# Two gate projections of a three-layer block as one tile, and weight rooms split into halves

## What is computed

```python
h = rmsnorm_2(x, g_mix)
proj = h @ w_in
fox_qkv, fox_f, sc_bcv, dn_qkv, dn_b, dn_a, dn_z, br_gate = split_cols(proj, IN_SIZES)
y_fox = forgetting_attention(fq, fk, fv, fox_f, b_fox_f, fox_q_gain, fox_k_gain)
#   log_f = log_sigmoid(f_logit + b_f); cum_f = cumsum(log_f); logits get cum_f[q] - cum_f[k]
y_sc = sb * causal_dwconv(sc * sv, sc_conv_w)
dn_qkv = silu(causal_dwconv(dn_qkv, dn_conv_w))
beta = sigmoid(dn_b)
g = -exp(dn_a_log) * softplus(dn_a + dn_dt_bias)
o_dn = gated_delta_rule(l2norm(dq), l2norm(dk_), dv_, g, beta)
```

## Time and profile before

| | us |
|---|---|
| three timed runs | 2346.04, 2346.47 (median), 2348.34 |
| profiled execution | 2348.38 |
| its span in the trace | 2345.5 |
| TensorE busy | 2289.0 (98%) |
| VectorE busy | 1129.4 (48%) |
| ScalarE busy | 870.5 (37%) |
| GpSimd busy | 386.5 (16%) |
| stage `mix` | about 1238 to 1310 |
| stage `fox` | about 1310 to 1374 |
| stage `dn` | 1374 to about 1635 |
| longest wait of TensorE for VectorE (line 1233, first block) | 6.0 |

### The profile page before, as it was taken

The page is one execution under the profiler, slowest core; times in us unless marked ns, Lnnn a source line. Parts: engine busy times, 40 slices in busy tenths (PEclk is TensorE's granted clock), DMA queues, the critical chain, the costliest instruction groups (busy, mean ns, idle before and its releaser), DMA issues.

```text
span 2345.5 us, 26129 instructions
## 1 busy us (share of the span) xinstructions
PE 2289.0 (98%) x10864; PEld 1855.9 (79%) x10864; DVE 1129.4 (48%) x1726; ACT 870.5 (37%) x1290; POOL 386.5 (16%) x339
## 2 busy tenths in 40 slices
PE   7899999999999999999999999999999999999998
PEld 6467888888876678888888878888888788888887
DVE  4974433434224645344346656554333346555553
ACT  5574221223224643122143465442322233333243
POOL 1431110112200012011031303332001111000020
PEclk9799999999999999999999999999999999999999
DMA  3303323223351022332346142225255332332332
GB/s 128 108 1 112 104 90 105 93 90 105 97 162 45 1 72 90 102 96 90 107 82 91 18 45 56 54 46 81 65 96 92 90 108 81 100 108 90 91 108 62
DMA packets 221955, 197.05 MB, mean 84 GB/s; under 512 B 5216, under 2 KB 215596, under 8 KB 221709
## 3 DMA queue, kind: packets, MB, share of 16 engines
q1 hardware_dynamic: 219820, 189.70, 30.8%
q0 software_dynamic: 1504, 5.51, 0.7%
q10 hardware_dynamic: 513, 0.17, 0.0%
HBM read 190.65 MB, written 4.72 MB: 83 GB/s over the span
## 4 chain that ended last, share of the span: by engine, by line
PE 90%; DVE 5%; ACT 3%; DMA 1%; issue 1%; ACTq 0%; POOL 0%; DVEq 0%; POOLq 0%
PE bank L525 24%; PE bank L527 24%; PE bank L526 24%; PE bank L2175 5%; PE bank L848 3%; PE bank L2361 2%; PE bank L1662 1%; PE bank L1489 1%; DVE dsa_latents L1179 1%; PE bank L699 1%; DVE small L1177 1%; PE bank L832 1%; PE bank L709 1%; PE bank L2052 1%; DVE weight_lo L511 1%; DMA weight_raw<-in_w_in 1%
## 5 line engine op out<-in xcount | busy, mean ns | idle before, releaser
L525 PE MATMUL bank<-h_hi,weight_hi 128*128 128x512 f32 x1576 | 619.6, 393 | 6.2 <-DVE h_lo L631 3.6
L527 PE MATMUL bank<-h_hi,weight_lo 128*128 128x512 f32 x1576 | 615.3, 390 | 0.0
L526 PE MATMUL bank<-h_lo,weight_hi 128*128 128x512 f32 x1576 | 614.9, 390 | 0.0
L511 DVE TENSOR_TENSOR weight_lo<-weight_raw,weight_hi 128x2048 fp32r<-128x2048 f32 (+2 forms) x182 | 385.0, 2115 | 382.6 <-ACT weight_hi L502 382.6
L502 ACT ACTIVATE weight_hi<-weight_raw 128x2048 fp32r<-128x2048 f32 (+2 forms) x183 | 321.4, 1756 | 359.2 <-PE bank L527 316.0
L525 PEld LDWEIGHTS bank<-h_hi,weight_hi 128*128 128x128 f32 x1576 | 296.4, 188 | 70.9 <-issue 7.4
L527 PEld LDWEIGHTS bank<-h_hi,weight_lo 128*128 128x128 f32 x1576 | 296.4, 188 | 63.1
L526 PEld LDWEIGHTS bank<-h_lo,weight_hi 128*128 128x128 f32 x1576 | 296.7, 188 | 61.7 <-issue 0.2
L525 PE MATMUL bank<-hidden_hi,weight_hi 128*128 128x512 f32 x512 | 201.8, 394 | 0.0
L527 PE MATMUL bank<-hidden_hi,weight_lo 128*128 128x512 f32 x512 | 200.7, 392 | 0.0
L526 PE MATMUL bank<-hidden_lo,weight_hi 128*128 128x512 f32 x512 | 198.7, 388 | 0.0
(11 more groups left out here) (411 smaller groups left out, 3155.1 us busy)
## 6 DMA issues: line engine op xcount, KB each, us to landing
weight_raw<-in_w_down SPq DMA_DIRECT2D x40, 1024.0 KB, 5.1
weight_raw<-in_w_up SPq DMA_DIRECT2D x32, 1024.0 KB, 5.4
weight_raw<-in_w_up SPq DMA_DIRECT2D x44, 512.0 KB, 5.1
weight_raw<-in_w_in SPq DMA_DIRECT2D x20, 1024.0 KB, 9.0
weight_raw<-in_w_in SPq DMA_DIRECT2D x26, 512.0 KB, 6.8
weight_raw<-in_w_kv_shared SPq DMA_DIRECT2D x6, 1024.0 KB, 5.0
weight_raw<-in_w_branch SPq DMA_DIRECT2D x6, 1024.0 KB, 5.0
weight_raw<-in_a_w_o SPq DMA_DIRECT2D x4, 1024.0 KB, 6.5
```

The source lines that it names most:

```text
L511: dve.e.tensor_tensor(split_flat(v, 1), raw_flat(v), f32(split_flat(v, 0)), ALU.subtract).then_inc(*split.mark(("unit", v)))
L525: pe.e.matmul(o, w[0], x[0], start=start, stop=False)
L526: pe.e.matmul(o, w[0], x[1], start=False, stop=False)
L527: return pe.e.matmul(o, w[1], x[0], start=False, stop=stop)
```

## The change

1. The unit and tile `dn_b` are gone. The unit `fox_f` now reads two ranges of 32 columns, `fox_f`'s and those of `dn_b` and `dn_a`, by two DMAs; its tile has 64 rows. Rows 0 to 7 are the forget gates, rows 32 to 39 the delta rule's.
2. In `mix`, ScalarE copies rows 32 to 39 out of PSUM, TensorE transposes them after fox tile 3, and VectorE multiplies them by the token factors of the norm (the projections of this stage are taken from the unnormed stream), to `ba_cols`. In `dn`, sigmoid and softplus start from `ba_cols`. The wait for the normed stream moves to the first delta rule tile.
3. `weight_raw`, `weight_hi` and `weight_lo` have four halves of 1,024 columns. `lay_out` gives a unit one or two halves in turn and lists the units that held them before; load and rounding wait for those. The loads have four semaphores instead of two, and a load also waits for unit u - 4.
4. At the start of `dn`, ScalarE and VectorE round and split up to the unit of ("dn", 0, 2) ahead of the softplus chain; before, up to that of ("dn", 0, 0).

The diff, cut to its core:

```diff
-    plan.insert(len(plan) - 5, (("fox_f", 0), (w, 0, NC, [(IN_F, IN_F + P)], True)))
-    add(("dn_b",), w, 0, NC, IN_B, IN_B + P)
+    plan.insert(len(plan) - 5, (("fox_f", 0), (w, 0, NC, [(IN_F, IN_F + 32), (IN_B, IN_B + 32)], True)))
...
-        raw_units = sbuf("weight_raw", P, N_RAW, UNIT_COLUMNS)
-        unit_pair = pair("weight", N_SPLIT, UNIT_COLUMNS)
+        raw_units = sbuf("weight_raw", P, N_RAW * UNIT_COLUMNS)
+        unit_pair = pair("weight", N_SPLIT * UNIT_COLUMNS)
...
-        raw_in = [signal(f"weight_in{n}") for n in range(N_RAW)]
+        raw_in = [signal(f"weight_in{n}") for n in range(2 * N_RAW)]
...
+        def lay_out(units, slots):
+
+
+            half_columns, at, last, where, before = UNIT_COLUMNS // 2, 0, [None] * (2 * slots), {}, {}
+            for u in units:
+                kc, width = unit_shape(u)
+                size = 1 if kc * width <= half_columns else 2
+                at = at + at % 2 if size == 2 else at
+                halves = [(at + n) % (2 * slots) for n in range(size)]
+                before[u] = sorted({last[n] for n in halves} - {None})
+                for n in halves:
+                    last[n] = u
+                where[u] = halves[0] * half_columns
+                at = (at + size) % (2 * slots)
+            return where, before
+
+        raw_at, raw_before = lay_out(range(len(plan)), N_RAW)
+        split_at, split_before = lay_out(halved, N_SPLIT)
...
-            if u >= N_RAW:
-                if plan[u - N_RAW][1][4]:
-                    sp.wait_ge(*split_by(u - N_RAW).when("unit", u - N_RAW))
+            for v in raw_before[u] + ([u - 2 * N_RAW] if u >= 2 * N_RAW else []):
+                if plan[v][1][4]:
+                    sp.wait_ge(*split_by(v).when("unit", v))
                 else:
-                    free, name = raw_free.get(u - N_RAW, (split, "none"))
+                    free, name = raw_free.get(v, (split, "none"))
                     sp.wait_ge(*free.when(*name))
...
-                    before = halved.index(v) - N_SPLIT
-                    act.wait_ge(*raw_in[v % N_RAW].when("unit", v))
-                    if before >= 0:
-                        act.wait_ge(*tile_full.when("unit", halved[before]))
+                    act.wait_ge(*raw_in[v % (2 * N_RAW)].when("unit", v))
+                    for before in split_before[v]:
+                        act.wait_ge(*tile_full.when("unit", before))
...
+        ba_rows, ba_cols = step(ATT + 15 * T, T)[32:40, :], small[:, 320:352].rearrange("p (t n) -> p t n", t=NT)
...
-            product_tile(pe, ("fox_f", 0), unit_at["fox_f", 0], 0, h_chunk, (mix.dve, ("forget",)))
+            u = unit_at["fox_f", 0]
+            bank = open_bank(pe, ("fox_f", 0), (mix.dve, ("forget",)), (mix.act, ("ba_rows",)))
+            pe.wait_ge(*split.when("unit", u))
+            for k in range(NC):
+                done = matmul3(pe, bank[0:64, :], columns(u, k, 0, 64), h_chunk(k), k == 0, k == NC - 1)
+            done.then_inc(*tile_full.mark(("fox_f", 0), ("unit", u)))
...
+                if t == 3:
+                    bank = open_bank(pe, ("ba",), (mix.dve, ("ba",)))
+                    pe.wait_ge(*mix.act.when("ba_rows"))
+                    for n in range(NT):
+                        done = pe.e.transpose(bank[:, 8 * n:8 * n + 8], ba_rows[:, n * P:(n + 1) * P], ident[32:40, 32:40])
+                    done.then_inc(*mix.pe.mark(("ba",)))
...
+            act.wait_ge(*tile_full.when("fox_f", 0))
+            act.e.activation(ba_rows, banks.of("fox_f", 0)[32:40, :], ACT.Copy).then_inc(*mix.act.mark(("ba_rows",)))
...
+            dve.wait_ge(*mix.pe.when("ba"))
+            dve.e.tensor_tensor(ba_cols, banks.of("ba")[:, 0:32].rearrange("p (t n) -> p t n", t=NT),
+                                mix_factor.unsqueeze(2).broadcast_to([P, NT, 8]), ALU.mult).then_inc(*mix.dve.mark(("ba",)))
...
+                if item == ("dn", 0, 0):
+                    pe.wait_ge(*fox.dve.when("h", k))
...
-            product(pe, ("dn_b",), h_chunk, lambda t: (dn.act, ("ba_rows",)), lambda k: (fox.dve, ("h", k)))
             tensor_slot(pe, ("open", 0))
-            bank = open_bank(pe, ("ba",), (dn.dve, ("x16",)), (dn.act, ("beta",)))
-            pe.wait_ge(*dn.act.when("ba_rows"))
-            for t in range(NT):
-                done = pe.e.transpose(bank[:, 8 * t:8 * t + 8], ba_rows[:, tiles[t]], ident[0:8, 0:8])
-            done.then_inc(*dn.pe.mark(("ba",)))
...
-            round_upto(act, unit_at["dn_b", 0] + 1)
-            act.wait_ge(*tile_full.when("dn_b", 0))
-            act.e.activation(ba_rows, banks.of("dn_b", 0)[0:8, :], ACT.Copy).then_inc(*dn.act.mark(("ba_rows",)))
+            round_upto(act, item_unit(("dn", 0, 2)))
             scalar_slot(act, ("open", 0))
-            act.wait_ge(*dn.pe.when("ba"))
-            act.e.activation(heads4(beta), banks.of("ba")[:, 0:32].rearrange("p (t n) -> p t n", t=NT)[:, :, 0:4], ACT.Sigmoid
-                             ).then_inc(*dn.act.mark(("beta",)))
+            act.wait_ge(*mix.dve.when("ba"))
+            act.e.activation(heads4(beta), ba_cols[:, :, 0:4], ACT.Sigmoid).then_inc(*dn.act.mark(("beta",)))
...
-            split_upto(dve, unit_at["dn_b", 0] + 1)
+            split_upto(dve, item_unit(("dn", 0, 2)))
             vector_slot(dve, ("open", 0))
-            ba = banks.of("ba")[:, 0:32].rearrange("p (t n) -> p t n", t=NT)
-            dve.wait_ge(*dn.act.when("beta"))
+            dve.wait_ge(*mix.dve.when("ba"))
             dve.wait_ge(*misc_in.when("dn_bias"))
-            dve.e.tensor_tensor(heads4(x16), ba[:, :, 4:8], dt_bias.unsqueeze(1).broadcast_to([P, NT, DN_HEADS]), ALU.add
+            dve.e.tensor_tensor(heads4(x16), ba_cols[:, :, 4:8], dt_bias.unsqueeze(1).broadcast_to([P, NT, DN_HEADS]), ALU.add
```

More of the change, by code:

```diff
@@ L450, in build_program @@
         halved = [u for u, (_, what) in enumerate(plan) if what[4]]
-        split_slot = {u: n % N_SPLIT for n, u in enumerate(halved)}
         raw_free = {}
@@ L456, in unit_shape, with raw_view @@
             return kc, sum(c1 - c0 for c0, c1 in ranges)
-        def raw_view(u):
-            kc, width = unit_shape(u)
-            return raw_units[:, u % N_RAW, 0:kc * width].rearrange("p (k n) -> p k n", k=kc)
+        def lay_out(units, slots):
[13 more added lines that the diff above has]
+        split_at, split_before = lay_out(halved, N_SPLIT)
         def raw_flat(u):
             kc, width = unit_shape(u)
-            return raw_units[:, u % N_RAW, 0:kc * width]
+            return raw_units[:, raw_at[u]:raw_at[u] + kc * width]
+        def raw_view(u):
+            return raw_flat(u).rearrange("p (k n) -> p k n", k=unit_shape(u)[0])
         def split_flat(u, half):
             kc, width = unit_shape(u)
-            return unit_pair[half][:, split_slot[u], 0:kc * width]
+            return unit_pair[half][:, split_at[u]:split_at[u] + kc * width]
         def columns(u, k, c0, c1):
@@ L485, in load_unit @@
                                w[r0:r0 + kc * P, c0:c1].rearrange("(k p) n -> p k n", p=P)
-                               ).then_inc(*raw_in[u % N_RAW].mark(("unit", u), by=16))
+                               ).then_inc(*raw_in[u % (2 * N_RAW)].mark(("unit", u), by=16))
                 at += c1 - c0
@@ L1041, in dsa_tensor @@
             u = unit_at["uk", 0]
-            pe.wait_ge(*raw_in[u % N_RAW].when("unit", u))
+            pe.wait_ge(*raw_in[u % (2 * N_RAW)].when("unit", u))
             for half in range(2):
@@ L1282, in up @@
                 pe.wait_ge(*att0.act.when("o_lat", h))
-                pe.wait_ge(*raw_in[uv % N_RAW].when("unit", uv))
+                pe.wait_ge(*raw_in[uv % (2 * N_RAW)].when("unit", uv))
                 pe.e.matmul(bank, raw_view(uv)[:, 0, h * P:(h + 1) * P], o_lat[h % 2], start=True, stop=True
@@ L2141, in build_program @@
         gcum, to_end, e_end, bexp = dnv[:, 128:144], dnv[:, 144:160], dnv[:, 160:176], dnv[:, 176:192]
-        ba_rows = Kd[:, 0].rearrange("p t n -> p (t n)")[0:8, :]
         ends = dnv[:, 224:240]
```

## The result

The changed kernel takes **2334.11 us** (median of four; 2331.5 to 2335.11), the kernel before 2346.41 beside it: ratio 0.9942, 95% interval 0.993 to 0.9955, some 12 us less. Beside other runs it took 2334.65 where before took 2347.17 (0.9948, 0.9935 to 0.9961). The profiled execution of after took 2331.5 us, span 2329.7; it is the fastest of its four, while that of before, 2348.38 us, stands above all four timed ones (2346.04 to 2348.34).

What follows compares the result with a forecast made beforehand. TensorE was taken as the bound, 90% of the last chain. An earlier `dn` chain (-11.1), moved transposes (+0.5) and full clock behind the remaining wait (-2.4) gave -13.0: 2333.5 us against the median, range 2330.8 to 2341.3.

Steps and rivals of the forecast that it cites:

- The tile and the gates: Opening of `dn`: the 24 matmuls of `dn_b`, 5.57 us on TensorE's path, vanish; the narrower `fox_f` tile costs nothing.
- The moved transposes: Four small transposes move from `dn` into the fox stage: -0.5 us there, +0.5 us here.
- The load of `fox_f`: Before the fox stage: two DMAs of 128 byte pieces land in 5.6 to 26.5 us; taken as no cost.
- The softplus chain: Opening of `dn`: `dt_bias` lands in 3.2 us, the chain runs 1379.5 to 1384.3, silu (0, 0) starts 11.1 us earlier.
- What is late next: Before ("sc", 0, 1): TensorE resumes 11.1 us earlier, at 1401.8, still waiting about 1.4 us instead of 2.73.
- The clock behind it: Behind the wait before ("sc", 0, 1): the granted clock holds instead of halving, another -2.4 us.
- A: The forecast itself: clock holds behind the remaining wait before ("sc", 0, 1), 2333.5 us; chance 0.46.
- B: Rival: the clock falls again behind the remaining wait, so only 10.6 us are saved, 2335.9 us; chance 0.27.
- the step that took the wait's length as what decides: Before ("sc", 0, 1): waits of 1.81 and 2.73 us brought half clock, one of 2.00 did not, so 1.4 should not.
- the one on the early layout: First block: `uv` and first `a_o` loads start earlier, meeting the bias transfer; TensorE's longest wait covers it; nothing taken.
- What halves are good for: Weight rooms in `dn`: four units loaded ahead instead of two, ending ScalarE's 3.59 us idle for the ("sc", 0, 0) load.
- rival C: `dn` chain no earlier relative to TensorE (late `dt_bias` DMAs or tap delayed by roundings); only tile matmuls go, 2341.1 us; chance 0.13.

Runs made afterwards that it cites:

- e10: The changed kernel itself, traced and timed again, nothing altered: 2334.65 us, ratio 0.9948 to the kernel before.
- e12: Changed kernel with the load of `fox_f` in eight DMAs of 1,024 pieces of 32 bytes instead of two of 128 byte pieces: 2335.21 us, one run.
- e5: Changed kernel with weight rooms in halves only from `fox_f` on, earlier units keeping whole slots: 2336.21 us, ratio 0.9955 to the kernel before.
- e11: Changed kernel with VectorE making the first branch's low halves earlier, between the second and third normed head: 2330.94 us, ratio 0.994 to the kernel before.
- e3: Changed kernel without the rounding ahead: one unit rounded and split at the opening of `dn` instead of three: 2335.41 us, ratio 0.9949 to the kernel before.
- e1: Changed kernel reduced to the merged gates: whole weight slots, only the first delta rule unit rounded ahead: 2341.86 us, ratio 0.9976 to the kernel before.
- e9: e1 with the two small DMAs of `a_log` and `dt_bias` issued one stage earlier, at the start of fox attention: 2341.62 us, ratio 0.9977 to the kernel before.

## Why the prediction was right, and where it was not

- **The tile and the gates.** -5.57 and nothing for the narrower tile: the 64 column matmuls take 389 to 397 ns. The moved transposes: +0.5 was said for the way from `mix` to `dn`; to the first tile of the stage it is 125.98 instead of 125.43 us, +0.55. ScalarE's copy took 0.59 us at 1257.24, the product 0.18, neither waited for.
- **The load of `fox_f`.** Two DMAs of 3.9 and 6.1 us, both landed 6.5 us behind the first issue, where 26.5 was the upper bound; TensorE didn't wait. "DMA: Bandwidth & Descriptors", Specifications, in the Trainium skill wants pieces of at least 512 bytes for full rate. The traces agree as to the rate: 512 KB in pieces of 512 bytes took 5.6 us, 256 KB in pieces of 128 bytes 6.5, in pieces of 32 bytes 16.3. What was too high was the prediction's reading that the load would near its upper bound by that rule.
- **The softplus chain.** Said: Abs 5.2 us behind the first tile, silu (0, 0) 13.1. Measured: 4.77 and 12.66; `dt_bias` landed in 2.7 us, not 3.2. The 1.38 us of drain of "ScalarE: Activation LUTs", What ACT_TABLE_LOAD costs, in the Trainium skill, show in no row: from Abs to the last Exp, 1377.03 to 1381.61, it is 4.58 us, with three loads of 1.28, as before.
- **What is late next.** Said: TensorE is there 26.1 us behind the first tile and waits 1.4. Measured: 27.07 - 0.91 = 26.16, and 0.91. The step held, and what it is off by is the landing of `dt_bias`: the wait is 0.88 to 0.97 us where that DMA took 2.7 to 2.8 us (after, e10, e12), and 1.44 and 1.57 where it took 3.3 and 3.4 (e5, e11). The prediction had 3.2 and 1.4.
- **The clock behind it.** Said: -2.4. From the end of that wait to the pair products it was 9.11 us, it is 6.70: -2.41. As A said, and not B; in the three traces with a wait of 0.9 (after, e10, e12) the clock held. But by the runs above, the step that took the wait's length as what decides was weak, and that A came and not B is in part luck: the wait of 1.33 us in e3 and that of 1.81 in the kernel before were followed by the fall, others up to 2.12 were not.
- **In all**, from `mix` to the sums, -13.3, where -13.0 was said.
- **The step that failed** is the one on the early layout: `uv` and the first `a_o` load "meet the transfer of the bias", the wait behind "covers it. I take nothing". The wait's end did stay at 112.1. What was not asked is what a shorter wait does to the clock behind it: 1.1 to 2.8 us.
- **What halves are good for.** The prediction gave them ScalarE's 3.59 us. e1 and e9 show more: with whole slots and `dn_b` gone, the load of ("dn", 0, 2), 11.2 us, is in flight when `dt_bias` is fetched, and rival C's delay, held unlikely because the DMAs "would have to be 5 us later than the row says", is nearly there (7.6 us, against the row's 3.2). In the changed kernel it did not happen: that load is issued at 1309, and the one in flight at 1374 is of ("sc", 0, 1), 6.8 us, and lands at 1375.8. The row of 3.2 was taken beside such a short load too; that another unit's load would stand there was not asked.
- 13.3 + 2.75 is more than the 12 to 13 us between the medians, and both traces are of executions at the edge, a slow one of before and the fastest of after. Single executions differ by falls of the clock of 1.7 us; that this makes the rest is argued, not shown. That the median came so near to 2333.5 is therefore in part luck: the sum from `mix` on was right, the gain in block 1 was missing from it, and the medians show less than the traces.

## What to carry to other kernels

When you remove work ahead of a prefetched chain, ask whether its loads are issued early enough for the new pace: alone, the removed tile turned at once into a wait of nearly the same length. Ask too which load will be in flight when a small DMA is issued, and how long that one takes. Read the clock behind each wait of TensorE together with the wait; shortening a wait whose end another engine sets can still pay, by the clock behind it. And look for operations like the four subtractions of `branch_lo` that stand behind the last step of a stage though their input has long been there.

## What was not expected of the hardware

- A fall of the granted clock behind a wait cost 1.5 to 1.8 us in most traces, in `dn`, in `merge` and in block 1 (2.8 to 3.1 behind the waits of 5.9 to 6.1 us in block 1 and once in `dn`), and came behind one and the same wait of 2.00 us in five traces of twelve.
- A DMA of 2 KB landed in 2.6 to 3.5 us beside a weight load of 512 KB that took 6.5 to 6.9 us, and in 5.6 to 7.6 us beside one that took 10.4 to 11.3; `dt_bias` landed 0.3 to 1.8 us behind that load in thirteen traces.
- Loads of the same size and shape (1,024 rows of 512 bytes) took 6.4 to 6.7 us or 10.7 to 11.6, by the unit they fetch: ("dn", 0, 1), where no other was in flight, the one, ("dn", 0, 2) the other.
- The same 256 KB landed within 6.5 us of the first issue in 2,048 pieces of 128 bytes, within 16.3 us in 8,192 pieces of 32 bytes.
